# Gated attention on one core: chunk states between the levels of the first half's scores, and the next head's pieces dealt out anew

## What is computed

```python
def gla_scan(q, k, v, log_a, s0, strict):
    def step(S, inp):
        qc, kc, vc, lac = inp
        b = jnp.cumsum(lac.astype(jnp.float32), axis=1)
        inter = jnp.einsum('bthk,bhkv->bthv', qc * jnp.exp(b), S)
        decay = jnp.exp(jnp.where(mask5, b[:, :, None] - b[:, None, :], -jnp.inf))
        scores = jnp.einsum('bthk,btshk,bshk->btsh', qc, decay, kc)
        intra = jnp.einsum('btsh,bshv->bthv', scores, vc)
        b_last = b[:, -1]
        S_new = jnp.exp(b_last)[..., None] * S + jnp.einsum(
            'bshk,bshv->bhkv', kc * jnp.exp(b_last[:, None] - b), vc)
        return S_new, inter + intra
...
def log_gate(lr, d):
    z = (lr @ gla_lr_w[d] + gla_lr_b[d]).astype(jnp.float32)
    return heads(jax.nn.log_sigmoid(z) / GLA_TAU, GLA_HEADS)
```

## Time and profile before

| what | us |
|---|---|
| median of three runs | 5284.6 (5282.94 to 5287.0) |
| run that was profiled | 5275.61 |
| its span, first to last instruction | 5273.7 |
| GLA heads 0 to 3, each from its first key pass to the next | 214.5, 215.0, 214.6, 139.7 |

### The profile page before, as it was taken

How to read it: one execution, slowest core, us unless ns; L and a number is a source line. 1 busy time by engine, 2 the same in 40 slices (tenths; PEclk the granted TensorE clock), 3 DMA queues, 4 the chain that set the end, 5 groups by cost and what they waited for, 6 DMA issues and landing times.

```text
span 5273.7 us, 47534 instructions
## 1 busy us (share of the span) xinstructions
PE 4471.8 (85%) x17532; PEld 2568.9 (49%) x17532; DVE 1907.3 (36%) x4174; ACT 1370.2 (26%) x3332; POOL 656.7 (12%) x833
## 2 busy tenths in 40 slices
PE   6898999897799998887777769977777899699993
PEld 3444665744346666354454453444454444544441
DVE  2434653723435536223343451021122102344444
ACT  3333551303234422132222321111221211122221
POOL 1021000201110002011232230011111000111113
PEclk8999999598899995978888979999889999599996
DMA  4002000122112202210000010000001001399993
GB/s 187 37 1 80 33 26 32 39 73 89 37 48 101 85 2 65 80 62 9 32 5 28 9 72 32 12 30 34 8 30 38 16 32 48 122 344 338 346 344 138
DMA packets 90213, 414.31 MB, mean 79 GB/s; under 512 B 10720, under 2 KB 42088, under 8 KB 69120
## 3 DMA queue, kind: packets, MB, share of 16 engines
q1 hardware_dynamic: 74144, 353.59, 18.8%
q0 software_dynamic: 15840, 57.68, 2.8%
HBM read 365.54 MB, written 45.69 MB: 78 GB/s over the span
## 4 chain that ended last, share of the span: by engine, by line
PE 79%; DVE 6%; ACT 5%; issue 4%; POOL 2%; DMA 2%; POOLq 0%; SPq 0%; DVEq 0%; ACTq 0%; PEldq 0%
PE psum L89 52%; PE psum L95 6%; PE psum L1723 4%; PE psum L877 3%; PE psum L856 3%; PE psum L1899 1%; ACT arena L938 1%; PE psum L1253 1%; PE psum L298 1%; DVE arena L403 1%; PE psum L1713 1%; PE psum L2333 1%; PE psum L1828 1%; PE psum L2296 1%; POOL arena L1940 0%
## 5 line engine op out<-in xcount | busy, mean ns | idle before, releaser
L89 PE MATMUL psum<-arena 128*128 128x512 f32 (+5 forms) x7208 | 2819.9, 550 | 81.9 <-ACT arena L2798 25.0
L89 PEld LDWEIGHTS psum<-arena 128*128 128x128 f32 x7208 | 1388.0, 200 | 1385.1 <-issue 1276.8
L95 PE MATMUL psum<-arena 128*128 128x128 f32 (+3 forms) x3020 | 492.1, 294 | 306.8 <-POOL arena L411 60.1
L95 PEld LDWEIGHTS psum<-arena 128*128 128x128 f32 (+3 forms) x3020 | 362.1, 148 | 517.4 <-issue 242.1
L176 DVE SCALAR_TENSOR_TENSOR arena<-psum,arena 128x512 f32<-128x512 f32 (+1 forms) x132 | 74.2, 562 | 530.0 <-ACT arena L173 528.8
L171 ACT ACTIVATE arena<-psum 128x512 f32<-128x512 f32 (+1 forms) x132 | 65.0, 492 | 681.9 <-PE psum L89 681.9
L1723 PE MATMUL psum<-arena 128*128 128x512 f32 (+1 forms) x480 | 232.7, 622 | 7.2 <-DVE arena L1694 5.8
L877 PE MATMUL psum<-arena 128*64 128x128 f32 x2624 | 202.5, 283 | 0.7 <-ACT arena L938 0.7
L856 PE MATMUL psum<-arena 64*128 64x512 f32 (+1 forms) x800 | 165.7, 544 | 16.3 <-ACT arena L945 8.4
L945 ACT ACTIVATE arena<-psum,arena 128x1280 f32<-128x1280 f32 (+1 forms) x144 | 175.9, 1232 | 10.0 <-DVE arena L905 7.7
L938 ACT ACTIVATE arena<-psum 128x512 f32<-128x512 f32 x200 | 112.7, 597 | 251.4 <-PE psum L95 251.4
(11 more groups left out here) (363 smaller groups left out, 4466.3 us busy)
## 6 DMA issues: line engine op xcount, KB each, us to landing
arena<-w_gu SPq DMA_DIRECT2D x47, 2048.0 KB, 8.8
arena<-w_ada SPq DMA_DIRECT2D x24, 2048.0 KB, 8.2
arena<-w_dn SPq DMA_DIRECT2D x47, 1024.0 KB, 9.1
arena<-w_in SPq DMA_DIRECT2D x12, 2048.0 KB, 10.2
yb_scratch<-arena POOLq DMA_DIRECT2D x47, 512.0 KB, 8.1
arena<-x_scratch SPq DMA_DIRECT2D x34, 512.0 KB, 6.2
arena<-w_out SPq DMA_DIRECT2D x6, 2048.0 KB, 8.8
arena<-gate_rows_scratch SPq DMA_DIRECT2D x36, 256.0 KB, 3.3
```

The costliest lines, as they stand in the source:

```text
L89: ins = e.matmul(out, l, r, start=(i == 0), stop=(i == n - 1))
L95: ins = e.transpose(o, i, idn)
```

## The change

The scores of the first half start one slot after the first keys: `mixed` advances the states' generator (`*_gla_states`, the first part of the old `*_gla_head`) at a "k" and the first half's scores at an "s", after a pattern of 20 slots. The turned keys use psum banks 3 and 4 instead of 0 and 1, which the diagonal and the levels use. `a_gla_soft` and the first two operations of `v_gla_decay` become one piece each, and the scans go two to a piece; the second direction starts six (ACT) and four (DVE) such steps after the first. `gla_pieces` deals the pieces out anew: 21 in the 20 mixed slots, then in each half's outputs 9, in the second scores 14. That is 53 of 56; before, all 56 were dealt out by the last slots.

```diff
+            soft = chain(a_gla_soft(e, h, 0), iter([0] * 6), a_gla_soft(e, h, 1))
...
-                    if (t, i) in ((2, 0), (3, 2)):
-                        a_gla_soft(e, h, t - 2)
+                    if t > 1:
+                        next(soft, None)
...
-            decays = (v_gla_decay(e, h, 0), v_gla_decay(e, h, 1))
+            decays = chain(iter([0] * 2), v_gla_decay(e, h, 0), iter([0] * 4), v_gla_decay(e, h, 1))
...
-                if c == 4:
+                if c % 2 and c < NT - 1:
                     yield
...
+        KEYS_IN_SCORES = "kskkskkskkskkskkskss"
+
         def gla_pieces(slot):
-            if slot < 12:
-                return 2 if slot in (0, 10) else 1
-            n = (slot - 12) % 26
-            if n < 8:
-                return 3 if n > 4 else 1
-            return 1 if n % 2 == 0 and n < 24 else 0
+            if slot < 20:
+                if KEYS_IN_SCORES[slot] == "k":
+                    return 1 if KEYS_IN_SCORES[:slot].count("k") < 6 or slot % 3 == 0 else 0
+                return 2 if slot > 12 else 1
+            slot -= 20
+            n = slot if slot < 18 else slot - 26
+            if n >= 0:
+                return 1 if n % 2 == 0 else 0
+            return 3 if n > -4 else 1
+
+        def mixed(keys, scores):
+
+            for x in KEYS_IN_SCORES:
+                next(keys if x == "k" else scores, None)
+                yield
...
-                e.activation(KDT[:, c0:c0 + n, :], P[c0 // 4 % 2][:, 0:n * 128].rearrange("p (c t) -> p c t", c=n), ACT.Copy
+                e.activation(KDT[:, c0:c0 + n, :], P[3 + c0 // 4 % 2][:, 0:n * 128].rearrange("p (c t) -> p c t", c=n), ACT.Copy
...
+        def pe_gla_head(e, h):
+            yield from mixed(pe_gla_states(e, h), pe_gla_scores(e, h, 0))
+            yield from stretches(pe_gla_out(e, h, c) for c in chunks_of(0))
+            yield from pe_gla_scores(e, h, 1)
+            yield from stretches(pe_gla_out(e, h, c) for c in chunks_of(1))
```

41 lines of the change are left out of this document (23 added, 18 removed).

## The result

| what | before, us | after, us |
|---|---|---|
| median of five runs each | 5282.94 (5277.06 to 5287.0) | 5302.72 (5297.97 to 5316.91) |
| span of the profiled run | 5273.7 | 5296.2 |
| GLA heads 0 to 3, from first key pass to first key pass | 214.3, 214.6, 215.0, 139.7 | 216.8, 218.5, 218.5, 148.3 |
| head 1 by the prediction's steps A, B, C, D | 110.9, 22.0, 60.5, 21.2 | 103.8, 22.9, 64.3, 27.5 |
| head 3, steps A to D | 63.8, 17.4, 40.3, 18.2 | 70.7, 19.0, 40.3, 18.2 |

The change makes the kernel slower: the ratio over all runs is 1.0044 (95% interval 1.0028 to 1.0061), and the medians differ by 19.8 us. The forecast was a gain, 5269.6 us with a range of 5241 to 5293; the measured time lies above both. In the profiles the four heads account for 18.5 of the 22.5 us between the spans: 2.5, 3.9, 3.5 and 8.6.

What follows compares the result with a forecast made beforehand. TensorE, 85% busy, was taken to bound the kernel through waits and half speed. A head of 99.5 + 20.6 + 63.8 + 24.6 = 208.5 us saves 6.5, three 19.5, less 4.5 in head 3: 5269.6 us, range 5241 to 5293.

Steps and rivals of the forecast that it cites:

- A: Head 1 from its start to the first output matmul (states and first-half scores): 99.5 us, before 110.9.
- B: Outputs of a head's first half, with 8 pieces instead of 7: 20.6 us, before 22.0.
- C: Scores of a head's second half, same 14 pieces at another place in a tile: 63.8 us, before 60.5.
- D: Outputs of the second half to the next head, eight pieces instead of five: 24.6 us, before 21.6.
- net of -15.0: Whole kernel: three heads save 19.5 us, head 3 costs 4.5 more; taken off the profiled span 5273.7 us.
- the half speed: Chopped stretch before level 5 in states and first scores: short bursts slow TensorE, 1.5 us added.
- Slower: Rival, chance 0.11: TensorE stays at half speed between turned keys and first output; 10 us more per head, 5299.6 us.
- The tail behind the last turn: Head's end: three pieces remain without cover; 3.44 us for two pieces, copies 0.95, turn 0.3, VectorE's copies 0.55.
- E: Head 3, nothing to fill with: first output at 68.3 us, before 63.8; levels wait 2.2 us in VectorE's queue.
- State updates beside GpSimd: VectorE's state updates beside GpSimd's products: 0.48 us each kept; at 1.55, eleven would add up to 11.8 per head.
- Twice the gain: Rival, chance 0.14: interleaving keeps TensorE at full speed and shrinks waits; 12 us more saved per head, 5233.6 us.
- No change: Rival, chance 0.29: half speed or VectorE-GpSimd collisions give back 2 to 5 us per head; 5280 us at 3.5.

Runs made afterwards that it cites:

- The added matmuls: Changed kernel plus sixteen 128x128 identity matmuls, read by nothing, ahead of each wait for the keys: 5289.95 against 5278.72 us for the kernel before, ratio 1.002.
- the kernel with four pieces: Changed kernel with four pieces instead of three in each of the last three slots of the second half's scores: 5304.85 us, ratio 1.0051 to the kernel before.
- interleaved kernel with early exponentials: Changed kernel with 28 pieces in the mixed slots, old dealing behind, ScalarE's exponentials a slot earlier, last head in old order: 5256.02 us, ratio 0.9951 to the kernel before.
- the old order: Kernel before with split decay passes, new banks, exponentials a slot earlier and 16 identity matmuls ahead of each wait for the keys: 5230.38 against 5279.63 us, ratio 0.991.

## Why the prediction was wrong

**The baseline.** Three heads of 215.0 made 645.0; the profile has 643.9 for heads 0 to 2. The net of -15.0 was taken off the profiled span, so the miss grows by these 1.1 us.

**A, forecast 99.5, measured 103.8.** The walk through the slots was right in its mechanism. Level 0 was put at 22.3 and came at 22.6; the waits before levels 0, 2 and 4 were to be 3.6 and are 3.62, 3.43 and 3.44; the keys between the levels cost 5.02 for 5.05. The step that failed is a term of the sum, the half speed. Level 0 to level 1 took 13.4 us instead of 11.7, with the gate projection at 5.22 (2630.33) for 3.5 at full speed; levels 5 to 6 took 7.3 instead of 4.4, since level 5 ran at 2.04 and two pieces at 5.61. I had "1.5 for half speed" there. This is the mechanism of the rival *Slower*, which I gave 0.11, at under half the 10 us per head that it needed; that its 5299.6 us came close to the measured 5302.72 is luck, since the rest came from B, D and head 3. The added matmuls, which act on half speed behind the waits for the keys alone, gave back 7.2 us in head 1, more than the 4.3 by which A was off. Against it I had argued that TensorE "recovered after the z pieces, within some 4 us of wider matmuls", which held after some waits and not after others: level 2 took 2.08 here and 1.16 in the kernel with four pieces, behind the same wait of 3.43. From such a walk the term can be had to some microseconds only.

**B, forecast 20.6, measured 22.9.** The step that failed is "the first Abs takes its place in time that ScalarE waited anyway". That held for the Abs. The Exp behind it did not: of ScalarE's timeline near the last chunk's gate,

```profile
2729.10 1.25 ACT L1654 ACTIVATE arena<-arena 128x1280 f32<-128x1280 f32 x1
2730.67 0.38 ACT L2047 ACTIVATE arena<-psum 128x256 f32<-128x256 f32 x1
```

the pass over 1280 columns stands right before the square of the last chunk's norm, and the last turn (2732.36 above) waits 1.82 us. I followed the first of three operations to its place and took the rest as free. (The prediction's bare work of 7.9 + 12.3 is 20.2; its 20.6 leaves 0.4 for waits.)

**C, forecast 63.8, measured 64.3.** Right in its main terms: the wait of 3.60 stands before level 4, and a second tile closes before level 6, with a wait of 2.35.

**D, forecast 24.6, measured 27.5.** The tail behind the last turn was forecast at about 5.2 (two pieces, copies, turn, copies) and is 5.9, from the last output turn (2818.51) to the next head's start (2824.39); four matmuls of 512 and two turns stand there as said. The sum was off as well: with 5.2 in place of the 1.2 us that stood behind the last turn before, 21.6 becomes 25.6 and not 24.6, as far as the prediction's sentences show. And what failed in the mechanism is that pieces in the last output slots "add nothing much". At 2801.19 a piece waits 2.19 us for VectorE's copy of the tile before it, and VectorE holds that copy behind the gate:

```profile
2800.32 0.42 DVE L2023 TENSOR_TENSOR arena<-psum,arena 128x256 f32<-128x256 f32 x1 [0.48 <-ACT arena L2042]
2800.86 0.28 DVE L1700 COPY arena<-psum 128x128 f32<-128x128 f32 x1
```

The projection bank comes free only then. I had priced the pieces by TensorE's time and not by the copy that stands in another queue behind a chain which itself waits.

**E, forecast 68.3, measured 70.7; head 3 +4.5 forecast, +8.6 measured.** The mechanism was right: level 1 is held back by VectorE's queue. TensorE's wait there is 2.10 as forecast (2.2), and VectorE's timeline shows what is ahead of the product (L1978):

```profile
3066.09 1.00 DVE L1854 SCALAR_TENSOR_TENSOR arena<-arena,psum 128x256 f32<-128x256 f32 x2 [4.73 <-PE psum L1844]
3067.12 0.42 DVE L1964 TENSOR_TENSOR arena<-arena 128x256 f32<-128x256 f32 x1
3067.47 0.42 DVE L1965 TENSOR_TENSOR arena<-arena 128x256 f32<-128x256 f32 x1
3067.80 0.69 DVE L1978 TENSOR_TENSOR arena<-arena 128x512 f32<-128x512 f32 x1
```

Two updates, two differences and the product, as the prediction listed them. The step that failed is again the clock: after the waits the gate projection takes 5.31 us (3077.11) instead of 3.5. The outputs of that half, whose first two chunks run at half speed, take 19.0 instead of 17.4 us, which the prediction did not count at all. On TensorE's side:

```profile
3068.59 1.13 PE L1915 MATMUL psum<-arena 128*128 128x128 f32 x8 [2.10 <-issue]
...
3077.11 5.31 PE L90 MATMUL psum<-arena 128*128 128x256 f32 x16
```

**The sum.** 4.3 + 2.3 + 0.5 + 2.9 make 10.0 us per head, 30.0 in three. Head 0 came 1.7 better than head 1, the baseline adds 1.1, head 3 4.1 and what lies outside the heads 4.0: 37.5 us, where the profiled spans give 5296.2 - 5258.7 = 37.5.

**State updates beside GpSimd.** The prediction kept 0.48 us for an update against 1.55 at the dear end. Of the nine backward updates in head 1 of the changed kernel only one ran beside GpSimd, in the timeline of VectorE and GpSimd:

```profile
2620.68 0.48 DVE L1854 SCALAR_TENSOR_TENSOR arena<-arena,psum 128x256 f32<-128x256 f32 x1
2620.78 0.61 POOL L1944 TENSOR_TENSOR arena<-arena 128x256 f32<-128x256 f32 x1
```

and in head 3 four more did, two of them beside its product (3104.32 and 3105.67, 0.48 each). So the term was rightly small in a filled head, and the overlap that it was about hardly occurs. The groups of VectorE's instructions in head 1 (form and count, busy us, mean ns of one, idle time before them) have a difference whose two inputs are both arena tiles:

```profile
L1965 DVE TENSOR_TENSOR arena<-arena 128x256 f32<-128x256 f32 x14 | 11.4, 811 | 0.0
```

It takes 0.81 us in the mean, where it took 0.42 in head 3's stretch above, with GpSimd idle. The Trainium skill, "SBUF — State Buffer", section "Who interferes with whom", has a VectorE instruction with at most one SBUF input free of contention with GpSimd and one with two inputs not; the trace agrees with both halves. One reading of the prediction was wrong: its product of 0.69 us "without" a GpSimd product did run beside one. VectorE's started at 2764.63 and GpSimd's at 2764.68, and there it was GpSimd's that took long, 1.77 us. Where GpSimd's started first (2700.41), it took 1.26 and VectorE's 1.79.

**The rivals and the chances.** *Twice the gain* was refuted by its own "against": the copy of a piece does stand ahead of the exponential, and moving the exponentials ahead was worth more than anything else that was tried. I had used it as a fixed price of both orders. That it could be removed by one line of ScalarE's program, and that the new order pays it more often than the old, would have been visible in the same rows. *No change* allowed for "2 to 5 us more per head" in A alone; the excess was 10, 4.3 of it in A and 5.2 in B and D, where a pass in ScalarE's queue and a copy in VectorE's had been set to nothing.

## What to carry to other kernels

In a chain across engines with queues in order, look for what stands in each queue directly ahead of the link, and move the link ahead of it, before interleaving two chains. Here each exponential queued a slot earlier gave 8 to 20 us a head, where the reordering of a whole stage gave nothing. And when filling work is dealt out anew, follow each piece through every queue that it passes, its copies too, since the bank that it frees is freed by the slowest of them. Where no other work fills the gaps, interleaved chains hold each other up in the queues that they share: head 3 paid 7.3 to 8.6 us.

## What the runs showed of the hardware

- With 16 matmuls of 128x128 in front of each wait for the keys, the work behind the first one ran at full speed in head 1 of the changed kernel: a z piece at 1.12 instead of 2.07 us, and 7.2 us less in A. In the interleaved kernel with early exponentials, work that nothing reads made the whole kernel faster (5256.02 to 5228.66 on the same chip).
- That added work is not free: the same 16 matmuls took 3.84 us with pieces right ahead of them, and 5.38 or 6.57 behind a wait of 2.9 us, and then they held up the work that they stand in front of by 0.8 and 1.9 us.
- Once at full speed, the z pieces fell back with no wait in front: 1.12 at 2599.41 and 2.07 at 2603.43 in the old order, 1.30 at 2599.53 and 2.07 at 2601.90 in the interleaved one. In the changed kernel with the added matmuls they stayed up to level 0 in head 1 and not in head 2. What decides stays open.
- The same wait of 3.43 us was followed by a level of 2.08 us in one kernel and 1.16 in another, at the same place of the order; in the changed kernel itself a wait of 3.60 was followed by 1.16. What decides between them stays open.
- When VectorE and GpSimd each multiply two arena tiles of 128x512 at the same time, the one that started first kept its time and the other took longer: 0.69 and 1.77 us with VectorE 0.05 ahead, 1.26 and 1.79 with GpSimd 0.02 ahead.
- Also open: whether VectorE's state update alone makes up the 3.5 us or more that interleaving costs with early exponentials (it was not moved by itself), and how the 2.8 to 3.7 us per head of the new dealing divide between the pieces and the places of the decay operations.
